# Transposes and index scores moved into the middle of the next unit, and a last token tile worked in column halves

## The reference

```python
proj = x @ w_in          # queries, keys, values of four branches; index q, k, w; 4 x 1024 gates
y_a = dsa_attention(...)           # top 128 keys by index score: sum_h relu(qi_h . ki) * wi_h
y_b = swa_sink_attention(...)      # window of 128, with a sink
y_c = moba_attention(...)
y_d = stick_breaking_attention(...)
merged = sum(sigmoid(g) * (y_n @ w_branch[n]))
h = layer_norm(ALPHA * x + merged @ w_out)
q = h @ wq                         # 8 heads, top 16 of 128 x 128 product keys
out = layer_norm(ALPHA * h + sum_e gate_e * gelu(h . u_e) * v_e)
```

## Time and profile before

| | |
|---|---|
| median of 3 runs | 1729.89 us (1728.78 to 1734.46) |
| profiled execution | 1732.18 us, its span 1730.4 us |
| PE busy | 1689.1 us, 98% of the span |
| DVE, POOL, ACT busy | 73%, 47%, 44% |
| share of PE in the chain that ended last | 88% |
| mean granted clock of PE | 0.995 |
| first stage (projections and attention) | to about 330 us |
| tail: last matmul to the end of the span | about 11 us |
| tail: ACT normalizes tile 3, full width | 1.24 us |

### The profile page before, as it was taken

The page is one execution under the profiler, slowest core; times in us unless marked ns, Lnnn a source line. Parts: engine busy times, 40 slices in busy tenths (PEclk is TensorE's granted clock), DMA queues, the critical chain, the costliest instruction groups (busy, mean ns, idle before and its releaser), DMA issues.

```text
span 1730.4 us, 24570 instructions
## 1 busy us (share of the span) xinstructions
PE 1689.1 (98%) x9061; PEld 1486.3 (86%) x9061; DVE 1255.8 (73%) x2490; ACT 768.7 (44%) x1301; POOL 820.7 (47%) x496
## 2 busy tenths in 40 slices
PE   7999999999999999999999999999999999999997
PEld 6667767778878999999999999999888888888886
DVE  2487896562353778789888987534888888888886
ACT  4444444522232443775577367534333333333332
POOL 5222222344446466766777677776433232332312
PEclk9999999999999999999999999999999999999998
DMA  5111111224233365899799789997999999999952
GB/s 200 61 62 50 59 60 54 77 94 146 84 112 110 113 197 186 306 372 345 253 333 384 249 286 386 383 364 296 405 390 354 384 376 351 383 372 354 389 190 85
DMA packets 126360, 417.65 MB, mean 241 GB/s; under 512 B 12961, under 2 KB 32417, under 8 KB 124705
## 3 DMA queue, kind: packets, MB, share of 16 engines
q1 hardware_dynamic: 70176, 232.81, 38.2%
q0 software_dynamic: 36864, 134.23, 20.6%
q10 hardware_dynamic: 19200, 49.03, 7.2%
HBM read 364.91 MB, written 50.86 MB: 240 GB/s over the span
## 4 chain that ended last, share of the span: by engine, by line
PE 88%; DVE 8%; ACT 2%; issue 1%; DMA 1%; POOL 0%; SPq 0%; another core or an unknown queue 0%; ACTq 0%; DVEq 0%; POOLq 0%
PE ps L1285 16%; PE ps L1287 16%; PE ps L1286 16%; PE ps L1514 11%; PE ps L1511 11%; PE ps L1512 11%; PE ps L1609 5%; PE ps L1370 1%; DVE dist_a L842 1%; DVE row L895 1%; DVE row L866 1%; DVE small L841 1%; PE ps L1395 1%; DVE small L892 1%; DMA raw<-w_units 0%
## 5 line engine op out<-in xcount | busy, mean ns | idle before, releaser
L1285 PE MATMUL ps<-tok_hi,w_hi 128*128 128x384 f32 (+2 forms) x1544 | 548.8, 355 | 8.4 <-issue 3.6
L1287 PE MATMUL ps<-tok_hi,w_lo 128*128 128x384 f32 (+2 forms) x1544 | 539.3, 349 | 0.0
L1286 PE MATMUL ps<-tok_lo,w_hi 128*128 128x384 f32 (+2 forms) x1544 | 539.3, 349 | 0.0
L539 ACT ACTIVATE w_hi<-raw 128x1024 fp32r<-128x1024 f32 x334 | 353.3, 1058 | 414.0 <-PE ps L1514 301.4
L486 POOL TENSOR_TENSOR w_lo<-raw,w_hi 128x1024 fp32r<-128x1024 f32 x128 | 318.2, 2489 | 165.8 <-ACT w_hi L539 165.2
L439 POOL TENSOR_TENSOR w_lo<-raw,w_hi 128x1024 fp32r<-128x1024 f32 x80 | 195.0, 2442 | 327.0 <-ACT w_hi L539 326.8
L1285 PEld LDWEIGHTS ps<-tok_hi,w_hi 128*128 128x128 f32 x1544 | 291.1, 189 | 35.7 <-issue 10.2
L1287 PEld LDWEIGHTS ps<-tok_hi,w_lo 128*128 128x128 f32 x1544 | 290.8, 188 | 18.6
L1286 PEld LDWEIGHTS ps<-tok_lo,w_hi 128*128 128x128 f32 x1544 | 291.3, 189 | 16.8
L1511 PE MATMUL ps<-w_hi,gh_hi 128*128 128x512 f32 x768 | 298.8, 389 | 0.0
L1512 PE MATMUL ps<-w_lo,gh_hi 128*128 128x512 f32 x768 | 298.8, 389 | 0.0
(11 more groups left out here) (208 smaller groups left out, 1866.9 us busy)
## 6 DMA issues: line engine op xcount, KB each, us to landing
raw<-u_units SPq DMA_DIRECT2D x128, 512.0 KB
raw<-v_rows SPq DMA_DIRECT2D x128, 512.0 KB
raw<-w_units SPq DMA_DIRECT2D x78, 512.0 KB
gate_d<-stage ACTq DMA_DIRECT2D x12, 2048.0 KB
gelu_d<-gelu_t ACTq DMA_DIRECT2D x120, 192.0 KB
gelu_in<-gelu_d SPq DMA_DIRECT2D x30, 768.0 KB
gate_in<-gate_d SPq DMA_DIRECT2D x28, 768.0 KB
gate_in<-gate_d SPq DMA_DIRECT2D x2, 1536.0 KB
```

What stands on the lines that cost most here:

```text
L539: act.activation(w_hi[:, n % RAW, :], raw[:, n % RAW, :], ACT.Copy).then_inc(hi_done, 1)
L1285: pe.matmul(out_, l_hi, r_hi, start=start, stop=False)
L1286: pe.matmul(out_, l_hi, r_lo, start=False, stop=False)
L1287: return pe.matmul(out_, l_lo, r_hi, start=False, stop=stop)
```

## The change

1. PE transposes a value unit n after the fourth of the eight chunks of unit n+1 (`after_unit`, called from `project` or from `fill_to`). Before, units 2, 7 and 8 were transposed after unit 3, and after unit 8 (both), and 13, 14, 20 at the end of unit n+1.
2. The index scores that stood after unit n stand in the middle of unit n+1, for n = 3 to 8; the last four so in the middle of unit 9.
3. ACT copies the transposes of unit n-1 inside `unit(n)`, between the split of weights and the read of unit n. Before, the copies of 7 and 8 stood ahead of the loop over the steps, the later ones behind the read.
4. Unit 9 is multiplied whole before scores(0) (half of it before); step -1 then does the first four chunks of unit 10, and the remaining 220 chunks go over 32 steps (before: 224, seven in each).
5. Tile 3's part of the last four units goes by column halves, each with a semaphore; DVE combines and takes statistics by halves, ACT normalizes, DVE scales and shifts, and SP stores by halves.

```diff
+FILL_FIRST = KC + 4
 def filled_by(s):
-    return 4 if s < -1 else KC + (KC * N_FILL - KC) * (s + 1) // N_ITEM
+    return FILL_FIRST + (KC * N_FILL - FILL_FIRST) * (s + 1) // N_ITEM
...
         @block.sync
-                else:
-                    sp.wait_ge(last_set, 1)
-                sp.dma_start(out[t * P:(t + 1) * P, :], x_tok[:, t, :]).then_inc(out_done, 16)
-            sp.wait_ge(out_done, 16 * NT)
+                    sp.dma_start(out[t * P:(t + 1) * P, :], x_tok[:, t, :]).then_inc(out_done, 16)
+            for a in range(2):
+                cols = slice(S * a, S * a + S)
+                sp.wait_ge(last_set, a + 1)
+                sp.dma_start(out[(NT - 1) * P:NT * P, cols], x_tok[:, NT - 1, cols]).then_inc(out_done, 16)
+            sp.wait_ge(out_done, 16 * (NT + 1))
...
         @block.scalar
             def unit(n):
-                if n + HI_AHEAD < U_END:
-                    split_hi(n + HI_AHEAD)
+                split_hi(n + HI_AHEAD)
+                if n - 1 in V_UNITS:
+                    v_to_tokens(n - 1)
                 projected(n)
...
-                if n == N_IDX:
-                    v_to_tokens(2)
                 if n >= N_IDX:
                     relu_scores(4 * (n - N_IDX))
-            v_to_tokens(7)
-            v_to_tokens(8)
...
                 for n in units_in(s):
                     unit(n)
-                    if n - 1 in V_UNITS and n - 1 >= N_FIRST:
-                        v_to_tokens(n - 1)
...
-            for t in range(1, NT):
+            for t in range(1, NT - 1):
                 finish_norm(t)
+            root(NT - 1, var2_set, std2_set)
+            act.wait_ge(shift_set, NT)
+            for a in range(2):
+                half = x_tok[:, NT - 1, S * a:S * a + S]
+                act.activation(half, half, ACT.Identity, scale=rstd[:, NT - 1:NT], bias=newton[:, NT - 1:NT])\
+                    .then_inc(norm2_set, 1)
...
         @block.vector
-                    dve.wait_ge(unit_done, U_END)
-                    add_sum(t)
+                    for a in range(2):
+                        half = x_tok[:, t, S * a:S * a + S]
+                        dve.wait_ge(last_full, a + 1)
+                        link(dve.scalar_tensor_tensor(half, half, ALPHA, ps[:, 2 * t + a, :], ALU.mult, ALU.add))
+                        link(dve.bn_stats(stats[:, t, a], half))
...
-            dve.wait_ge(norm2_set, NT)
-            last_tile(ln2_gt, ln2_bt, last_set)
+            for a in range(2):
+                cols = slice(S * a, S * a + S)
+                half = x_tok[:, NT - 1, cols]
+                dve.wait_ge(norm2_set, NT + a)
+                link(dve.tensor_tensor(half, half, ln2_gt[:, cols], ALU.mult))
+                dve.tensor_tensor(half, half, ln2_bt[:, cols], ALU.add).then_inc(last_set, 1)
...
         @block.tensor
-            def project(n, bank):
+            def project(n, bank, midway=lambda: None):
...
+                    if c == 3:
+                        midway()
...
+            def after_unit(n):
+                if n in V_UNITS:
+                    if n == V_ORDER[0]:
+                        pe.wait_ge(consts, 1)
+                    v_to_tokens(n)
+                if N_IDX <= n < N_FIRST:
+                    index_scores(4 * (n - N_IDX))
...
             def att_unit(n):
                 att_ready(n)
-                project(n, n % 2)
+                project(n, n % 2, lambda: after_unit(n - 1))
...
-                if n == N_IDX:
-                    pe.wait_ge(consts, 1)
-                    v_to_tokens(2)
-                if n >= N_IDX:
-                    index_scores(4 * (n - N_IDX))
-            v_to_tokens(7)
-            v_to_tokens(8)
...
                     filled[0] += 1
+                    if c == 3:
+                        after_unit(n - 1)
                     if c == KC - 1:
                         last.then_inc(unit_done, 1)
-                        if n - 1 in V_UNITS and n - 1 >= N_FIRST:
-                            v_to_tokens(n - 1)
-            fill_to(filled_by(-2))
+            fill_to(KC)
...
+            def last_halves(first, t, operands, column):
+                tile_ = slice(column * P, (column + 1) * P)
+                for a in range(2):
+                    o, cols = ps[:, 2 * t + a, :], slice(a * S, a * S + S)
+                    for k in range(RAW):
+                        s, (l_hi, l_lo) = (first + k) % RAW, operands(k)
+                        last = three(o, l_hi[:, tile_], l_lo[:, tile_], w_hi[:, s, cols], w_lo[:, s, cols],
+                                     False, k == RAW - 1)
+                    last.then_inc(last_full, 1)
...
-            last_units(U_END - RAW, range(1, NT), lambda k: pe.wait_ge(gh_lo_set, P - RAW + k + 1),
+            last_units(U_END - RAW, range(1, NT - 1), lambda k: pe.wait_ge(gh_lo_set, P - RAW + k + 1),
                        lambda k: (gh_hi[:, k, :], gh_lo[:, k, :]), ffn_full, lambda t, k: None, 1)
+            last_halves(U_END - RAW, NT - 1, lambda k: (gh_hi[:, k, :], gh_lo[:, k, :]), NT - 2)
```

More of the change, by code:

```diff
@@ L309, in peer_block @@
     gelu_back = [sem(f"gelu_back{i}") for i in range(2)]
-    gh_set, gh_hi_set, gh_lo_set, var2_set, std2_set, out_set, shift_set = (sem(n) for n in (
-        "gh_set", "gh_hi_set", "gh_lo_set", "var2_set", "std2_set", "out_set", "shift_set"))
+    gh_set, gh_hi_set, gh_lo_set, var2_set, std2_set, out_set, shift_set, last_full = (sem(n) for n in (
+        "gh_set", "gh_hi_set", "gh_lo_set", "var2_set", "std2_set", "out_set", "shift_set", "last_full"))
     def wait_lo(engine, n):
@@ L978, in norm @@
                 add(t)
-                dve.bn_stats(stats[:, t, 0], x_tok[:, t, 0:S])
-                link(dve.bn_stats(stats[:, t, 1], x_tok[:, t, S:DM]))
+                if not (on_act and t == NT - 1):
+                    dve.bn_stats(stats[:, t, 0], x_tok[:, t, 0:S])
+                    link(dve.bn_stats(stats[:, t, 1], x_tok[:, t, S:DM]))
                 link(dve.bn_aggr(mean_var[:, t], stats[:, t]))
```

## The result

The changed kernel takes 1736.72 us in the median of 6 runs (1735.47 to 1739.15), the kernel before 1729.72 (6 runs, 1728.51 to 1734.46): a ratio of 1.0036, 95% interval 1.0022 to 1.0050. The forecast was 1736.2 in a range of 1730.5 to 1739.5. The profiled execution took 1737.18 us, its span is 1735.4, 5.0 above the span before.

What follows compares the result with a forecast made beforehand. PE, busy 98% of the span, bounds the kernel. First third +7.4 us (17.45 added, 10.07 removed), tail -1.1: +6.3 on the median 1729.89 makes 1736.2 us, range 1730.5 to 1739.5.

Steps and rivals of the forecast that it cites:

- The heart: Ahead of unit 10: PE waits 4.9 us because ACT copies unit 8's transposes only behind exponents(0); half clock adds 1.65.
- The five waits: PE stops for ACT's copies ahead of units 9, 10, 15, 16, 22: 1.5, 4.9, 2.5, 2.0, 1.0 us.
- the faster rival: ACT's copies of units 8, 13, 14 come before PE needs them: sum -8.1 us, 1721.8; chance 0.12.
- What goes: PE's waits after units 3, 8, 14, 15, 21 and half clock behind the first two vanish: 10.07 us.
- Clock: Half clock follows the waits ahead of units 10, 15 and 16, 1.65 us each; none at units 9 and 22.
- clock stays up at unit 16: Rival: no half clock behind unit 16's wait, waits at 15 and 16 near the low end: 1734.6 us; chance 0.18.
- One sign that I had named as "wrong": After PE waits of 2 us and more, a clock staying at 1.00 would speak against the forecast.
- Step 0 and DVE: Step 0 has 6 chunks instead of 7, so PE comes 0.7 us earlier and waits 0.6 us for DVE's probabilities.
- a rival in which DVE gives time back: PE's stalls let DVE run ahead, returning up to 5.8 us, mostly steps 16 to 23: about 1730.4; chance 0.09.
- The sum: Whole kernel: 17.45 us added against 10.07 removed, first third +7.4, tail -1.1, together +6.3 us.
- Tail: After PE's last matmuls, tile 3 by halves gains 1.1 us (0.8 to 2.1): statistics 0.7, normalization 0.2, store 0.2.
- The half-width combine: DVE's combine of half of tile 3, in the tail: taken as 0.7 us, between half of 1.22 and 0.8.

Runs made afterwards that it cites:

- E1: Changed kernel, but ACT copies unit 8's transposes ahead of the last four rectified index scores instead of behind exponents(0): 1733.64 us, 1.0016 of the kernel before.
- E2: Changed kernel, but ACT copies the transposes of units 13, 14 and 20 at the end of the step that makes them: 1733.31 us, 1.0016 of the kernel before.
- E3: Changed kernel with ACT's copies of units 7, 8, 13, 14 and 20 all made early: 1727.84 us, 0.9983 of the kernel before.
- F3: Changed kernel, copies of units 7, 8, 13, 14, 20 early, POOL's weight remainders held beside DVE's search and its merge pass behind DVE's addition: 1715.07 us, ratio 0.9924.
- G1: Kernel before, with POOL's weight remainders held until beside DVE's search and its merge pass held behind DVE's addition: 1723.75 us, ratio 0.9965.
- F2: Kernel before, with only POOL's one pass in the merge held behind DVE's addition: 1729.78 us, ratio 0.9999.
- F4: Kernel before, with only unit 2's transposes moved mid unit 3 and the first four index scores mid unit 4: 1727.51 us, ratio 0.9989.
- F1: Changed kernel, with POOL's weight remainders in the first steps held until beside DVE's search: 1732.04 us, 1.0013 of the kernel before.
- G2: Changed kernel, with POOL's weight remainders held until beside DVE's search and its merge pass behind DVE's addition: 1730.02 us, 0.9999 of the kernel before.
- E4: Kernel before, with only the last tile's column halves (part 5 of the change): 1728.99 us, ratio 0.9998.

## Why the prediction was right, step by step

**The heart holds.** The five waits were forecast as 1.5, 4.9, 2.5, 2.0 and 1.0 us, 11.9 in all; they came as 1.26, 4.56, 2.24, 1.82 and 0.75, 10.6. With the 0.2 us ahead of scores(0) that the 4.9 includes, each is about 0.2 short. E1, E2 and E3 show the cause: with ACT's copies moved, and PE's order left as it is, the waits go one by one. E3 is also the faster rival made true by an edit; in the change itself the copy stands where the program puts it. Priced at 8.1 us below the kernel before, it gave 2.7 in E3, and 8.5 where POOL is held in both kernels (F3 against G1), though these early copies also spare the waits of units 9 and 22.

**What goes.** All 10.07 us of waits and half clock went in the profile. Unit 4's index scores start at 35.52 without a wait (I had 35.3).

**Clock.** I gave 1.65 us each to the waits of units 10, 15 and 16. Units 10 and 15 took 1.9 and 1.7; unit 16 took nothing. That rival (clock stays up at unit 16) came true as a mechanism; at 1.82 us the wait is also shorter than the 1.88 that was the shortest with a fall. The rule of the Trainium skill that I weighed with it ("TensorE: Matmul & The Clock Gate", Part 4: PE-mode transpose), that transposes don't count as busy the way matmuls do, is neither borne out nor refuted here: in F2 and G1 four transposes stand directly ahead of an idle of 1.85 and 1.82 us, as they do ahead of the 1.88 of the kernel before, and the clock stays at 1.00. One sign that I had named as "wrong", a clock at 1.00 after 2 us and more, did not come in the changed kernel, but it came behind the 2.51 us of F2 and F4: my 1.65 us for such a wait of the kernel before hold in some executions and not in others.

**Step 0 and DVE** is the term that was mis-sized: 0.6 us, measured +1.3 (7.1 against 5.8). I reasoned that DVE is simply done later than PE comes. In truth the division had run into POOL's pass, and F1 shows that this is where all of it comes from. I also read the 5.8 us of before as DVE's own chain and made of them a rival in which DVE gives time back; the opposite came, and G1 shows that they too are POOL's: with the pass held, none is left and 6.2 us are gained.

**The sum.** Front: waits 10.6 and the 0.2 ahead of scores(0), clock 3.6, DVE 1.3, less 10.07, makes +5.6; the branch starts 6.13 later. Some 0.5 us has no row of mine (entries into the units, small idles below what the views list). I had +7.4. Tail -1.1, as forecast in its sum, but of other parts: 0.8 where I had 0.7 for the statistics, -0.3 where I had 0.2 for the normalization (POOL's pass again), 0.6 where I had 0.2 for the store. The half-width combine, for which I had no row, took 0.68. In the profiles that is +5.0, in the medians +7.0. The 2.0 between them is the step from profile to median: I carried the 2.3 us by which the profiled execution of before stood above the median over to the changed kernel, whose profile stands only 0.5 above. The runs offer the reason. The 2.51 us wait fell to half clock in three profiles of five and the 1.9 us wait in two of four, so the median of before holds less than the 3.3 us of clock that I removed; the waits of units 10 and 15 fell in every profile that has them, four each. So two errors of 1.3 and 1.8 us with opposite signs make the median come out within 0.5 us; that closeness is luck, the mechanism is not. Which share of the runs falls isn't known, as only profiled executions show their clock.

**Left open:** what decides whether the clock falls after an idle of 1.9 to 2.5 us, and how often the merge takes its longer course. The profiles do say what F2's hold can give. From the branch's start to the product in the merge, seven profiles take 28.53 to 28.57 us (those in which the clock fell at the 2.35 us wait), the four with the 4.22 us take 30.14, and G2, where the clock stayed up as in these four but the pass is held, takes 28.56. So the hold is worth 1.6 us in the longer course and nothing in the other, which F2's own profile took. That F2 gains nothing in the median fits a kernel before that mostly takes the shorter course, and the 2.0 us of G2 below F1 fit the 1.6; neither is shown, as only profiled executions tell the course.

## What to carry to other kernels

When work is moved on one engine, look at where the engine that frees its buffer does its part: here PE's transposes came half a unit earlier and ACT's copy one chain later, and 14.2 of the 15.7 us that the change added are in that (waits of 10.6 and clock of 3.6). The edit that paid was on neither: a pass of POOL moved from beside DVE's arithmetic to beside its search was worth 6 us on the kernel before and 10 to 12 (by ratios, by medians) on the version with the copies early, which had 10.3 us of these waits against 5.8: each wait removed ahead of them had brought PE to the next one sooner. A wait that a profile lays to an engine may be that engine's wait for another one: compare the duration of the last instruction with its twin elsewhere in the trace before taking it for a chain.

## What the runs showed of the hardware

**POOL's two-input pass stops some of DVE's instructions and not others.** Stopped were the division (0.61 to 2.12 us for two instructions), an addition (0.69 to 2.27), the first scaling of the tail (0.68 to 1.16), a 128x2 scalar operation (0.17 to 2.00, in E1 at 79.33) and one of 128x512 in the kernel before (0.43 to 2.17 at 268.88). The search is not. Timeline of F3, POOL's held pass and DVE's search beside it:

```profile
83.90 0.42 DVE L864 MAX8 small<-dist_a 128x8 f32<-128x256 f32 x1
...
84.08 2.42 POOL L448 TENSOR_TENSOR w_lo<-raw,w_hi 128x1024 fp32r<-128x1024 f32 x1 [3.57 <-DVE small L900]
...
84.88 0.43 DVE L864 MAX8 small<-dist_a 128x8 f32<-128x256 f32 x1
...
85.87 0.43 DVE L864 MAX8 small<-dist_a 128x8 f32<-128x256 f32 x1
```

The Trainium skill, "SBUF — State Buffer", "Who interferes with whom", says that a DVE instruction with at most one input in SBUF, outside the modes that use a second port, doesn't contend with GpSimd, and that of two that do contend the one issued first holds the shared ports for its whole instruction while the other is blocked. The durations here agree: the division of E1 that began at 84.39, beside a pass from 83.75 to 86.09, ended at 86.51, and the addition of E4 ended at 359.38, 0.55 behind a pass that began before it. Which mode the division runs in, no run here shows.

**The clock after a wait of about 2 us is not settled by the program.** The same wait with the same instructions ahead of it: behind 1.88 and 1.86 us the clock fell (before, E4), behind 1.85 and 1.82 not (F2, G1); behind 2.51 us it fell before, in E4 and G1, not in F2 and F4; 2.35 us ahead of the branch's last product fell in seven profiles of twelve. 1.8 us ahead of unit 16 didn't fall in any of four, 2.24 us and 4.56 us fell in four of four each. Of the 27 falls in the twelve profiles between 20 and 370 us, 24 cost 1.4 to 1.9 us (by the granted clock over the 8 us behind the wait) and three 2.7 to 3.0: unit 10 in G2, where the chunks took 5.38 us instead of 4.72, and the merge in E3 and F1. So one profile is off by 2 to 3 us from another of the same kernel for this alone.
